# Prompt queries and probabilities turned by plain transposes that write their PSUM tile from the last column to the first

## The chip, the cores and the metric

The kernel runs on one NeuronCore of one Trainium2 chip. The metric is the device time of one execution in microseconds (us), lower is better; the number that stands for a kernel is the median of several runs.

## What is computed

One inference step of a hybrid decoder layer, on 256 prompt tokens and 64 sample tokens (8 sequences of 8), with a model width of 2048, all in float32. Cut to what matters here:

```python
z = einsum("bsd,dc->bsc", rms_norm(x, g_mix), w_in)      # one wide projection
q, k = rms_norm(z_q, g_qb), rms_norm(z_k, g_kb)          # 16 heads of 64
# attention of the prompt, patterns (window, dilation) = (128,1), (512,4), (2048,16)
sc = einsum("brnqhe,brnkhe->brnhqk", q, k) * scale + bias[t5_bucket(distance)]
p  = exp(sc - max(sc)); o = einsum("...qk,...ke->...qe", p / sum(p), v)
# sample tokens: the same against a cache of 2048 past keys and values
# further: gMLP spatial gate, cross-attention into 256 memory tokens
h  = x + concat(ya, yb, ym) @ w_out
y  = h + hier_moe(rms_norm(h, g_ffn))                    # top-1 of 4 groups, top-2 of 8 experts
```

The bias of the window attention depends only on the distance between query and key.

## The kernel before, in words

The program is written engine by engine; each engine runs its instructions in the written order and waits on semaphores. There are three stages. First the memory projection. Then a loop over `UNITS_X` = 108 units `s` of the input projection (nine chunks of 512 columns, four quarters of the weights each, three row groups), with all attention work hung between the units at fixed places. Last the output projection and the mixture of experts, whose weights are streamed through a ring.

The projections use a seven-product scheme per 2x2 block: TensorE runs `plain_products` and `mixed_products` (L620) for the prompt rows and `small_unit` (L612) for the sample rows; VectorE mixes the weights (L1408 to L1424) and adds the products (L1435 to L1446). Weight blocks come over the SP queue (L402), cached keys and values too (L467, L472).

Attention needs operands turned (transposed). `turn(n)` is called 24 times: `kind = n // 4` says what is turned (0 memory keys, 1 and 3 prompt and sample queries, 2 and 4 keys, 5 memory queries), `w` which 128 columns. For kinds 1 and 3 the two tiles of prompt queries (`t < 2`) must come out with the queries in reverse order, because the window bias is read from memory by a DMA whose rows step forwards by one element while the distance has to fall; so the scores have their query rows reversed, and the probabilities are reversed back when `pair_turn` turns them. Scalar engine copies each turned tile out of PSUM (L1225 for `turn`, L1239 for `pair_turn`).

In the kernel before, a reversing turn is an ordinary matmul with the data as left operand and the constant `flip`, the identity with its rows in reverse order, as right operand. A turn without reversal is `nc.tensor.transpose` with the identity (here `tr`). A group of heads is handled in pairs: `pair_scores(p)` at `s = PAIR_AT[p]`, `pair_turn(p)` two units later, `pair_values(p)` three units later; the sample sequences are handled by `qk` (L780, L786), `turn_s` (L796) and `pv` (L813). The places are given by two tables:

```python
PAIR_AT = (37, 41, 45, 49, 71, 75, 79, 83)
TURN_AT = [10, 11, 12, 13, 19, 20, 21, 22, 30, 31, 32, 33, 61, 61, 62, 62, 66, 66, 67, 67, 91, 91, 92, 92]
```

Of the kernel before, what the change touches and what calls it, by code (L numbers as in the profile page):

```python
# [29 lines left out]
P = 128  # L30
# [40 lines left out]
def sample_step(s):  # L71

    for n, at in enumerate(START):
        if at <= s < at + 7:
            return n, s - at
    return None, None
# [17 lines left out]

CST = {}
_at = 0
for _n, _w in (("ident", 128), ("gx", 16), ("flip", 128), ("ones", 128), ("ltri", 128), ("iota", 64),
               ("gmix", 16), ("gmem", 16), ("bs", 4), ("bss", 4), ("gff", 16), ("wr", KT * 36), ("wst", 4 * 128), ("wsbd", 4 * 64),
               ("wmask", 256), ("wsel", 32), ("mmask", 512), ("msel", 32)):
    CST[_n] = (_at, _w)  # L100
    _at += _w
# [19 lines left out]
def hybrid_step(nc, x_rows, mem_rows, x_t, mem_t, w_proj, w_o, kc, vc, mkc, mvc, cst_d, gv_d,  # L121
                relb_d, onehot_d, w_gu, w_dn, mst_d, o_y, o_k, o_v, o_va, o_mk, o_mv,
                bias_d, bias_q_d):
    with ExitStack() as ctx:
        def sb(name, shape, dt=F32):
            return ctx.enter_context(nc.sbuf_tensor(name, shape, dt))
# [5 lines left out]
        cst = sb("cst", [P, NCST])  # L132
# [5 lines left out]
        ps = ctx.enter_context(nc.psum_tensor("ps", [P, 8, 512], F32))  # L138

        def c(name, rows=P):  # L140
            a, w = CST[name]
            return cst[0:rows, a:a + w]

        def area(at, *dims):
            n = int(np.prod(dims))
            ap = arena[:, at:at + n]
            if len(dims) == 1:
                return ap
            names = "abcdef"[:len(dims)]
            return ap.rearrange(f"p ({' '.join(names)}) -> p {' '.join(names)}",  # L150
                                **{k: v for k, v in zip(names, dims)})

        ident = c("ident")
# [54 lines left out]
        sc_p = [area(A_SP + 512 * b, 512) for b in range(3)]  # L208
# [42 lines left out]
        def field(t, at, *dims):  # L251
            n = int(np.prod(dims))
            names = "abcdef"[:len(dims)]
            return t[:, at:at + n].rearrange(f"p ({' '.join(names)}) -> p {' '.join(names)}", **{k: v for k, v in zip(names, dims)})
# [4 lines left out]
        pw = field(cst, done + 6 * P + 1024, 3, P)  # L259
        pwT = field(cst, done + 6 * P + 1024, NT)  # L260
        assert done + 9 * P + 1024 <= NCST
        pm = field(cst, CST["flip"][0], 3, P)
        actT = field(stat, 184, 2, SLOTS)

        mst = gv[:, 0:NMST]
# [328 lines left out]
        def _(pe):  # L594
            mm, tr = nc.tensor.matmul, nc.tensor.transpose
# [58 lines left out]
            for k in range(K4):  # L654
                pe.wait_ge(w_first[k], 16)
                pe.wait_ge(mem_scaled, k + 1)
                for t in range(2):
                    last = mm(ps[:, t, :], memT[:, k, t * P:(t + 1) * P], wring[:, 0, k, :], start=k == 0, stop=False)
                    if k == K4 - 1:
                        last.then_inc(unit_done, 1)  # L660
            for i in range(1, 2 * QTR):
# [9 lines left out]
                if i == QTR - 1:  # L671
                    pe.wait_ge(s_relb, 32)
                    for n in range(4):
                        last = mm(ps[32 * n:32 * n + H, 6, :], relb[:, :], onehot[:, n * 512:(n + 1) * 512], start=True, stop=True)
# [3 lines left out]
            pe.wait_ge(s_cst, 32)  # L678
            pe.wait_ge(tab_cp, TABLE // 512)

            def turn(n):
                kind, w = n // 4, n % 4
                pe.wait_ge(normed, (1, 2, 3, 4, 5, 6)[kind])
                if n == 0:
                    pe.wait_ge(z_ready, 4)
                if n == 12:
                    pe.wait_ge(y_used, 4)
                if n == 20:
                    pe.wait_ge(y_used, 8)
                if n >= 2:  # L690
                    pe.wait_ge(tr_used, n - 1)
                for t in range(2 if kind == 0 else 3):
                    if kind == 0:
                        src = mk[:, t, w * P:(w + 1) * P]
                    else:
                        src = z[:, (Z_QK, Z_KQ, Z_QK, Z_KQ, Z_QM)[kind - 1], t, w * P:(w + 1) * P]
                    if kind in (1, 3) and t < 2:
                        last = mm(ps[:, 3 + n % 2, t * P:(t + 1) * P], src, c("flip"), start=True, stop=True)
                    else:
                        last = tr(ps[:, 3 + n % 2, t * P:(t + 1) * P], src, ident)  # L700
                last.then_inc(tr_done, 1)

            def pair_scores(p):
# [11 lines left out]
            def pair_turn(p):  # L715

                pe.wait_ge(sc_read, 2 * p + 2)
                for k in range(2):
                    pe.wait_ge(p_ready, 2 * p + k + 1)
                    for a in range(0, 384, 128):  # L720
                        last = mm(ps[:, 3 + k, a:a + 128], sc_p[k][:, a:a + 128], c("flip"), start=True, stop=True)
                    last.then_inc(pt_mm, 1)

            def pair_values(p):
# [155 lines left out]
            for s in range(UNITS_X):  # L880
                ch, q, t = s // 12, s // 3 % QTR, s % 3
# [10 lines left out]
                n, i = sample_step(s)  # L892
# [41 lines left out]
                for p, at in enumerate(PAIR_AT):  # L934
                    if s == at + 2:
                        pair_turn(p)
                for k, at in enumerate(TURN_AT):
                    if s == at:
                        turn(k)
# [57 lines left out]
            for t in range(3):  # L997
                last = tr(ps[:, 7, t * 36:(t + 1) * 36], lgT[:, t * P:(t + 1) * P], ident[0:36, 0:36])
# [376 lines left out]
        def _(dve):  # L1375
# [113 lines left out]
            def squares_of(k):  # L1489
                src, groups, e, _, scratch, need = norms[k]  # L1490
                if k == 1:
                    dve.wait_ge(po, 2)
                if k == 5:
                    dve.wait_ge(st_v[0], 32)
                    dve.wait_ge(spv_mm, 12)
                    dve.wait_ge(pv_mm, 4)
                dve.wait_ge(z_ready, need)
                V.tensor_tensor(scratch, src, src, ALU.mult).then_inc(squared, 1)

            def sums_of(k):  # L1500
                _, groups, e, _, scratch, _ = norms[k]
                dve.wait_ge(squared, k + 1)
                link(V.tensor_reduce(st_n[:, 0:groups], scratch.rearrange("p n (h e) -> p (n h) e", e=e), X, ALU.add))
                V.tensor_scalar(st_n[:, 0:groups], st_n[:, 0:groups], 1.0 / e, EPS, ALU.mult, ALU.add).then_inc(ms_ready, 1)  # L1504
                state["n"] += 1

            def scale_by_root(k):
                src, groups, e, _, _, _ = norms[k]
                dve.wait_ge(rs_ready, state["n"])
                hh = COLS // e  # L1510
                for t in range(src.shape[1]):
                    v = src[:, t].rearrange("p (h e) -> p h e", e=e)
                    last = V.tensor_tensor(v, v, st_nr[:, t * hh:(t + 1) * hh].unsqueeze(2).to_broadcast([P, hh, e]), ALU.mult)
                last.then_inc(rooted, 1)
# [499 lines left out]
def distance_bucket(dist):  # L2014

    d = np.maximum(dist, 0)
    exact = 16
    df = np.maximum(d, 1).astype(np.float32)
    large = exact + (np.log(df / np.float32(exact)) / np.float32(math.log(2048 / exact)) * np.float32(16)).astype(np.int32)
    return np.where(d < exact, d, np.minimum(large, 31))  # L2020


def constants():

    dist = DIST0 - np.arange(TABLE)
    count = sum(((dist >= 0) & (dist <= w) & (dist % dl == 0)).astype(int) for w, dl in ((128, 1), (512, 4), (2048, 16)))
    onehot = np.zeros((33, TABLE), np.float32)
    onehot[distance_bucket(dist), np.arange(TABLE)] = 1
    onehot[32] = np.where(count > 0, np.log(np.maximum(count, 1)), NEG)
    c = {n: np.zeros((P, w), np.float32) for n, (_, w) in CST.items()}  # L2030
    c["ident"][:] = np.eye(P)
    c["flip"][:] = np.eye(P)[::-1]
    c["ones"][:] = 1
    c["ltri"][:] = np.triu(np.ones((P, P)), 1)
    c["iota"][:] = np.arange(64)
    h, q = np.divmod(np.arange(P), NQ)
    c["wmask"][:] = (h % 4)[:, None] == np.arange(256) // DH
    c["wsel"][:] = h[:, None] // 4 * NQ + q[:, None] == np.arange(32)
    b, h = h // G, h % G
    c["mmask"][:] = h[:, None] == np.arange(512) // DG  # L2040
    c["msel"][:] = b[:, None] * NQ + q[:, None] == np.arange(32)
    m = np.zeros((P, NMST), np.float32)
    m[:, 0:128] = np.arange(1, 129)
    m[:, 128:160] = (np.arange(P) % 32)[:, None] == np.arange(32)
    m[:, 160:160 + NTHR] = SLOTS * np.arange(1, NTHR + 1)
    return onehot, c, m
# [86 lines left out]
```

## Time and profile before

| | |
|---|---|
| median of 3 runs | 1121.97 us (1121.44 to 1122.15) |
| the profiled execution: its time | 1128.33 us |
| the profiled execution: its span | 1126.4 us |
| TensorE matmul busy | 1039.1 us, 92% of the span |
| VectorE busy | 546.9 us, 49% |
| ScalarE busy | 202.6 us, 18% |
| mean granted TensorE clock | 0.986 of full speed |
| DMA | 384.54 MB, mean 341 GB/s |

The span is the time from the first to the last instruction of the profiled execution. Shares of busy time are averages over stages with different limits, so they have to be read with the stage in mind: the input projection with the attention lies from about 100 to 500 us, the output projection from about 500 to 665 us, the experts after that.

### The profile page before, as it was taken

Reading aid. Unit: us, or ns where it says so; the run is one execution under the profiler, and the core shown is the slowest. Engines: PE = TensorE matmul, PEld = TensorE weight load, DVE = VectorE, ACT = ScalarE, POOL = GpSimd, SP = SyncE. Lnnn points to the kernel's source line nnn. Section 1 sums busy time; section 2 is a strip of 40 time slices with the busy share of each in tenths; the row PEclk is TensorE's granted clock in tenths of the full one; section 3 lists DMA queues with packets and bytes.
Section 4 is the critical chain, followed back from the end, with each engine's and each line's share of the span. In section 5 each row is a group of like instructions: output and inputs, shape, how many; then the busy total and the mean of one; then the engine's idle time right before and its main releaser. Section 6 shows DMA issues by size and latency. Waiting matters only on the chain.

```text
span 1126.4 us, 17412 instructions
## 1 busy us (share of the span) xinstructions
PE 1039.1 (92%) x7225; PEld 589.5 (52%) x7225; DVE 546.9 (49%) x1076; ACT 202.6 (18%) x463; POOL 43.1 (4%) x40
## 2 busy tenths in 40 slices
PE   8998999999999999999999998998996879787887
PEld 3686876666666666677777543333332323232232
DVE  3765555555544566475534135544443434343432
ACT  1022103131212331311101112121211111111112
POOL 0030110001100000000000000000000000000000
PEclk9998999999999999999999999999999999998999
DMA  9899648989999999733957459999999999999995
GB/s 323 341 280 262 246 152 350 358 338 348 352 415 410 380 358 367 306 143 119 336 216 279 169 221 388 429 415 428 427 428 427 427 429 428 429 428 427 427 426 223
DMA packets 38981, 384.54 MB, mean 341 GB/s; under 512 B 4911, under 2 KB 7599, under 8 KB 10895
## 3 DMA queue, kind: packets, MB, share of 16 engines
q1 hardware_dynamic: 36336, 375.83, 83.4%
q0 software_dynamic: 1568, 5.62, 2.0%
q10 hardware_dynamic: 1008, 2.10, 0.5%
q8 instruction: 52, 0.85, 0.3%
q14 instruction: 17, 0.14, 0.0%
HBM read 375.63 MB, written 7.90 MB: 340 GB/s over the span
## 4 chain that ended last, share of the span: by engine, by line
PE 68%; DMA 20%; DVE 7%; ACT 2%; issue 2%; POOL 0%; SPq 0%; ACTq 0%; DVEq 0%; POOLq 0%
PE ps L620 24%; DMA arena<-w_gu 15%; PE ps L612 7%; PE ps L1092 6%; PE ps L1019 5%; PE ps L1130 4%; PE ps L813 4%; PE ps L1111 3%; PE ps L602 3%; PE ps L780 3%; DMA arena<-x_rows 3%; DMA arena<-w_proj 2%; DVE cst L1900 1%; PE ps L1135 1%; PE ps L796 1%
## 5 line engine op out<-in xcount | busy, mean ns | idle before, releaser
L620 PE MATMUL ps<-arena 128*128 128x256 f32 x1456 | 333.7, 384 | 4.4 <-DVE arena L1435 4.4
L620 PEld LDWEIGHTS ps<-arena 128*128 128x128 f32 x1456 | 272.3, 191 | 53.4 <-issue 17.3
L1092 PE MATMUL ps<-arena,cst 128*32 128x512 f32 x1024 | 127.0, 631 | 30.7 <-DMA arena<-w_gu 29.1
L1900 DVE STREAM_TRANSPOSE cst<-ps 128x512 f32<-128x512 f32 x31 | 22.2, 717 | 177.0 <-PE ps L1019 177.0
L612 PE MATMUL ps<-arena 128*64 128x256 f32 x832 | 101.3, 385 | 0.0
L1092 PEld LDWEIGHTS ps<-arena,cst 128*32 128x32 f32 x1024 | 32.3, 113 | 115.8 <-issue 77.9
L1019 PE MATMUL ps<-arena,cst 128*32 128x512 f32 x768 | 90.6, 605 | 0.5 <-DVE cst L1829 0.5
L1111 PE MATMUL ps<-arena,stat 128*32 128x512 f32 x512 | 61.6, 598 | 23.3 <-DVE stat L1904 23.2
L612 PEld LDWEIGHTS ps<-arena 128*64 128x64 f32 x832 | 55.1, 136 | 38.5 <-issue 15.4
L1408 DVE TENSOR_TENSOR arena<-arena 128x512 f32<-128x512 f32 x52 | 35.7, 687 | 54.7 <-PE ps L620 39.5
L1930 DVE COPY arena<-ps 32x512 f32<-32x512 f32 x62 | 42.9, 691 | 38.7 <-PE ps L1111 37.4
L1019 PEld LDWEIGHTS ps<-arena,cst 128*32 128x32 f32 x768 | 26.0, 115 | 63.9 <-issue 62.6
L1130 PE MATMUL ps<-arena,cst 128*128 128x512 f32 x112 | 49.9, 598 | 9.2 <-ACT cst L1365 9.2
L1892 DVE TENSOR_TENSOR arena<-ps,arena 128x512 f32<-128x512 f32 x64 | 44.0, 691 | 20.9 <-PE ps L1130 18.4
L1340 ACT COPY gv<-ps 128x512 f32<-128x512 f32 x32 | 18.7, 585 | 188.2 <-PE ps L1092 188.2
L602 PE MATMUL ps<-arena 128*128 128x512 f32 x112 | 49.7, 596 | 1.2 <-DMA arena<-w_proj 0.8
L1362 ACT COPY arena<-ps 32x512 f32<-32x512 f32 x62 | 35.6, 575 | 76.9 <-PE ps L1111 76.1
L1101 PEld LDWEIGHTS ps<-gv 128*128 128x128 f32 x256 | 31.1, 191 | 26.5 <-issue 26.0
L1963 POOL TENSOR_TENSOR stat<-stat,nhalf 128x24 f32<-128x24 f32 (+4 forms) x10 | 26.6, 2655 | 477.4 <-DVE stat L1504 324.0
L813 PE MATMUL ps<-arena 128*32 128x256 f32 (+1 forms) x704 | 44.0, 383 | 0.1
L780 PE MATMUL ps<-arena 128*32 128x512 f32 (+1 forms) x384 | 39.3, 527 | 0.9 <-issue 0.6
L1424 DVE TENSOR_TENSOR arena<-arena 128x512 f32<-128x512 f32 x52 | 36.0, 692 | 6.4 <-PE ps L620 2.3
(286 smaller groups left out, 973.0 us busy)
## 6 DMA issues: line engine op xcount, KB each, us to landing
arena<-w_gu SPq DMA_DIRECT2D x64, 2048.0 KB, 29.6
arena<-w_dn SPq DMA_DIRECT2D x32, 2048.0 KB, 28.5
arena<-w_proj SPq DMA_DIRECT2D x43, 1024.0 KB, 7.8
arena<-kc SPq DMA_DIRECT2D x16, 2048.0 KB, 10.3
arena<-vc SPq DMA_DIRECT2D x16, 2048.0 KB, 9.6
arena<-w_o SPq DMA_DIRECT2D x16, 1024.0 KB, 4.9
arena<-kc SPq DMA_DIRECT2D x8, 1024.0 KB, 9.1
arena<-vc SPq DMA_DIRECT2D x8, 1024.0 KB, 10.0
```

The lines of the kernel that those rows point to most:

```text
L602: last = mm(ps[:, bank + t, :], src[:, kt, r0:r0 + m], wring[:, i % SLOTS_W, k, :], start=first and k == 0, stop=final and k == K4 - 1)
L612: last = mm(ps[64 * j:64 * j + 64, bank, col:col + HALF], src[:, kt, NPROMPT:NT], wring[:, i % SLOTS_W, k, HALF * j:HALF * j + HALF], star ...
L620: last = mm(psum[:, regions(v)[j - 1]], left[a], right[:, a], start=first and opens and a == 0, stop=final and a == 1, skip_group_check=True)
L780: last = mm(ps[32 * g:32 * g + 32, 6, 0:w], qpad[:, e * 128 + 32 * g:e * 128 + 32 * g + 32], kp[j][:, e, :], start=half == 0, stop=half == 1)
L813: last = mm(ps[32 * g:32 * g + 32, 5, 0:256], pt_s[0:w, t, 32 * g:32 * g + 32], v, start=t == 0, stop=t == VT)
L1019: last = mm(ps[32 * j:32 * j + 32, 1, :], pm[:, t, 32 * s:32 * s + 32], hres[:, t, 512 * j:512 * j + 512], start=t == 0, stop=t == 2)
L1092: last = mm(ps[g:g + 32, 0, :], xgT[:, s % 2, kt, :], w[:, k, :], start=kt < 4, stop=kt >= KT - 4)
L1111: last = mm(ps[32 * g:32 * g + 32, 3, :], actT[:, j, :], w[:, j, 512 * g:512 * g + 512], start=j == 0, stop=j == 1)
L1130: mm(ps[:, 4 + n, :], pwT[:, t * P:(t + 1) * P], y4[:, 512 * n:512 * n + 512], start=True, stop=True).then_inc(comb_mm, 1)
L1424: V.tensor_tensor(wmix[:, 3], b21, wmix[:, 1], ALU.subtract).then_inc(w_mixed, 1)
L1892: V.tensor_tensor(yres[:, t, cols], ps[:, bank + n, :], before[:, t, cols], ALU.add).then_inc(added[t], 1)
L1930: V.tensor_copy(y4[32 * b:32 * b + 32, 512 * g:512 * g + 512], ps[32 * g:32 * g + 32, 3, :]).then_inc(ye_copied, 1)
```

## The change

The reversing matmuls are replaced by transposes with the identity, and the reversal moves to where the result is written: `backward(bank, a)` builds an access pattern for the same 128 columns of PSUM that starts at the last column and has a step of -1. The constant `flip` is no longer made; its place among the constants stays (now `slots`, zeros), since a later tensor (`pm`) lies there. No instruction is added, dropped or moved on any engine, and no wait changes: the engines issue the same calls in the same order, and only the form of 64 calls on TensorE is another.

```diff
-for _n, _w in (("ident", 128), ("gx", 16), ("flip", 128), ("ones", 128), ("ltri", 128), ("iota", 64),
+for _n, _w in (("ident", 128), ("gx", 16), ("slots", 128), ("ones", 128), ("ltri", 128), ("iota", 64),
...
-        pm = field(cst, CST["flip"][0], 3, P)
+        pm = field(cst, CST["slots"][0], 3, P)
...
+            def backward(bank, a):
+
+                (step, rows), (one, _) = ps[:, bank].ap
+                return bass.AP(tensor=ps[:, bank].tensor, offset=ps[:, bank].offset + a + P - 1, ap=[[step, rows], [-one, P]])
...
-                    if kind in (1, 3) and t < 2:
-                        last = mm(ps[:, 3 + n % 2, t * P:(t + 1) * P], src, c("flip"), start=True, stop=True)
-                    else:
-                        last = tr(ps[:, 3 + n % 2, t * P:(t + 1) * P], src, ident)
+                    out = backward(3 + n % 2, t * P) if kind in (1, 3) and t < 2 else ps[:, 3 + n % 2, t * P:(t + 1) * P]
+                    last = tr(out, src, ident)
...
-                        last = mm(ps[:, 3 + k, a:a + 128], sc_p[k][:, a:a + 128], c("flip"), start=True, stop=True)
+                        last = tr(backward(3 + k, a), sc_p[k][:, a:a + 128], ident)
...
-    c["flip"][:] = np.eye(P)[::-1]
```

## Rows read from the trace of the kernel before

**Rows 1.** The page: busy time by engine, and the span in 40 slices

```profile
PE 1039.1 (92%) x7225; PEld 589.5 (52%) x7225; DVE 546.9 (49%) x1076; ACT 202.6 (18%) x463; POOL 43.1 (4%) x40
...
PE   8998999999999999999999998998996879787887
...
DMA  9899648989999999733957459999999999999995
```

**Rows 2.** Stretches: us, busy by engine, granted clock, DMA share, GB/s

```profile
98.00:105.00 7.00, 4.89 (x12) 3.94 (x13) 5.06 (x9) 4.16 (x9) 0.88 (x1) 0.51 1.00 290
105.00:645.00 540.00, 534.49 (x3896) 377.17 (x3895) 285.47 (x597) 108.23 (x283) 29.36 (x17) 1.00 0.78 300
645.00:690.00 45.00, 39.99 (x247) 18.35 (x249) 20.07 (x84) 8.28 (x18) 0.88 (x1) 1.00 0.62 247
690.00:1120.00 430.00, 369.14 (x2715) 130.10 (x2708) 178.50 (x290) 68.46 (x140) 0.00 (x0) 0.97 0.98 416
```

**Rows 3.** The chain that ended last, in order: start, us, what (around reversing turns)

```profile
125.49 0.45 PE ps L698 x4
125.94 0.11 PE ps L700
126.05 1.88 PE ps L612 x16
...
194.41 1.34 PE ps L721 x12
195.75 3.46 PE ps L620 x16
...
490.44 0.11 PE ps L754
```

**Rows 4.** All matmuls of three lines: duration min/median/max in ns, first and last start

```profile
L698 PE MATMUL ps<-cst,arena x32: 272/275/377, 125.3 to 306.3; 128*128 128x128 f32 x32
L721 PE MATMUL ps<-cst,arena x96: 275/275/377, 194.2 to 422.6; 128*128 128x128 f32 x96
L700 PE MATMUL ps<-cst,arena x52: 272/273/330, 93.1 to 456.2; 128*128 128x128 f32 x52
```

**Rows 5.** TensorE in order of time: start, length of the group, count

```profile
166.51 0.49 PE L700 MATMUL ps<-cst,arena 128*128 128x128 f32 x3
166.84 0.60 PE L620 MATMUL ps<-arena 128*128 128x256 f32 x2
324.20 0.88 PE L700 MATMUL ps<-cst,arena 128*128 128x128 f32 x6 [0.55 <-DVE arena L1529]
324.92 0.60 PE L620 MATMUL ps<-arena 128*128 128x256 f32 x2
```

**Rows 6.** The chain where it leaves TensorE, from 142 and from 245 us

```profile
135.72 0.11 PE ps L700
...
140.93 1.31 PE ps L620 x6
...
148.04 4.17 POOL stat L1963
...
155.53 1.82 DVE arena L1529 x3
...
157.39 0.55 PE ps L700 x3
...
245.34 0.06 PE ps L713
...
252.63 0.61 DVE arena L1585
...
253.38 1.92 PE ps L780 x16
255.30 1.53 PE ps L721 x12
256.84 3.46 PE ps L620 x16
```

**Rows 7.** VectorE mixing weights beside the turn at 255 us

```profile
254.66 0.69 DVE L1424 TENSOR_TENSOR arena<-arena 128x512 f32<-128x512 f32 x1
```

**Rows 8.** Keys loaded at 305 us, their landing, and their first matmuls

```profile
305.09 11.98 SPq L467 DMA_DIRECT2D arena<-kc  x3
...
DMA to landing us min/median/max: 10.7/13.7/14.0
...
L780 PE MATMUL ps<-arena x48: 379/592/617, 321.7 to 333.7; 128*32 128x512 f32 x32, 128*32 128x256 f32 x16
```

**Rows 9.** The experts: first loads on the SP queue, and the chain's longest pieces

```profile
664.65 0.80 SPq L531 DMA_DIRECT2D arena<-w_dn  x2
668.36 0.33 SPq L529 DMA_DIRECT2D arena<-w_gu  x1
...
1077.45 28.00 DMA arena<-w_gu
```

## The prediction

> **What bounds the kernel now.** I read the page first: TensorE is busy 92% of the span, and its slices stand at 9 in nearly all of the first two thirds, while the DMA slices reach a steady 9 only in the last third [rows 1]. So the limit changes on the way, and the next view is the table of stretches. From 105 to 645 us TensorE is busy 534.49 of 540 us at full clock, with DMA at 0.78: that stretch is bound by TensorE. From 690 to 1120 us DMA is at 0.98 and TensorE at 369 of 430 us: that one is bound by the expert weights [rows 2]. All reversing turns lie from 125 to 423 us [rows 4], so in the first kind of stretch. The chain that ended last confirms it: it goes through the very matmuls that the change edits, both in `turn` (L698) and in `pair_turn` (L721) [rows 3]. What they get shorter by is on the path there.
>
> **What the change does, step by step.** The edited calls are 64: in `turn`, kinds 1 and 3 are eight turns with two reversed tiles each, 16 tiles; `pair_turn` is called eight times with six tiles each, 48 tiles. The trace shows 32 matmuls for the 16 calls of L698 and 96 for the 48 calls of L721, so an ordinary float32 product of a tile runs as two passes. L700, a transpose, shows 52 matmuls for its 8 + 8 + 36 calls: one pass each [rows 4].
>
> Price of a pass. The duration of one is 272 to 275 ns in both forms [rows 4], but passes overlap, so what counts is the distance from one to the next. Reversing: 12 passes of L721 take 1.34 us of the chain, 4 passes of L698 take 0.45 us: 112 ns each, 224 ns a tile [rows 3]. Transposing: from the first of three L700 to the matmul behind them 166.84 - 166.51 = 0.33 us, 110 ns a tile, and a single L700 or L754 stands with 0.11 us in the chain [rows 3, 5]. The six at 324.20 us take 0.72 us to the next matmul, 0.12 us each, the first of them straight behind a wait [rows 5]. I take 109 to 110 ns a tile.
>
> The sum: a pair turn goes from 1.34 to 6 x 0.109 = 0.65 us, 0.69 us less, times 8 is 5.5 us. A query turn goes from 0.45 + 0.11 to 3 x 0.109 us, 0.23 us less, times 8 is 1.85 us. Together 7.3 us, or 64 x 115 ns. Nothing else has a cost: no instruction and no wait is added, the constants have the same size, and the copies L1225 and L1239 read the same columns.
>
> The unknown term is the write from the last column to the first; no row of the trace has one. Bounds: below, 109 ns a tile, as the forward transposes; a gain beyond that is excluded, since the same columns are streamed. Above I take twice that, 218 ns, each written column costing two steps instead of one; 64 x (224 - 218) leaves 0.4 us of gain. All rows of passes have about 0.85 ns a column, in either form and with the plain product delivering sums instead of moved data, so the pace follows what is streamed in, and the order in which addresses are counted out looks like a matter of one number in the pattern. I take the lower bound.
>
> The Trainium skill (TensorE: Matmul & The Clock Gate, Part 4, PE-mode transpose) gives about 275 ns for a transpose inside a kernel. The trace agrees as far as the duration of a single one goes, 273 ns. Were that the cost in the stream, the sum would be 64 x (224 - 275), 3.3 us slower; the distance of 110 ns between neighbours says that it is not.
>
> **Does it arrive at the end?** Where the chain leaves TensorE, I looked at what started the detour and whether a reversing turn lies in its shadow. From 142 to 157.4 us it runs over VectorE and GpSimd (square sums, the power on GpSimd at 148.04, the scaling L1529) and begins behind a matmul of L620 that ends at 142.24 us; the query turns before it are done by 135.8 us, so it only begins earlier. From 245.3 to 253.4 us it runs over VectorE, from the scores L713 to the keys' product L780; the turn at 255.30 us comes behind it [rows 6]. Next late could be the mixing of weights on VectorE: the pair turn at 255 us is followed by products that want the blocks of L1424, whose last ends at 255.35 us, while the turn would end at 256.84 - 0.69 = 256.15 us: 0.8 us are left [rows 6, 7]. That one is the closest I found; I allow 0.1 us for such small waits. The keys of 305 us are the tightest load: the first lands about 14 us after 305.09, at 319.1 us at the latest, and is used at 321.7 us [rows 8]. Between issue and use lie at most two query turns (the last at 306.3 us [rows 4]) that shrink by 0.46 us together, against 2.6 us of slack. The issue itself waits for TensorE and moves with it.
>
> The expert stage does not get shorter, it starts earlier. Its stream of loads starts with the issues at 664.65 and 668.36 us, which wait for TensorE's use of the ring and for the router's work, and before them DMA is not full (0.62 from 645 to 690 us) [rows 2, 9]. So it begins some 7 us sooner and ends as much sooner.
>
> The profiled execution took 1128.33 us with a span of 1126.4; less 7.3 it would be 1121.0. The median of the runs is 6.36 us below it, which no row divides; I carry the saving over whole: 1121.97 - 7.3 = 1114.7 us, 0.65% faster. A measurement of this kernel tells about 0.2% (2.2 us) from no change.
>
> **Rivals.** (1) Part of the gain is hidden: a VectorE chain or a load takes over after some of the turns. For it speaks that VectorE's mixing ends only 0.8 us ahead at 255 us, and DMA is at 0.78 on average [rows 2, 7]; against it that I found slack at each place. If a third to a half of the pair turns' 5.5 us goes to new waits, 1116.5 to 1117.5 us; at the worst 1119.5. Chance 0.09.
>
> (2) The backward write costs a second step a column: 218 ns a tile, 1121.6 us, no change. Nothing in the profile shows it or excludes it. Chance 0.08.
>
> (3) The other side: the backward write breaks the stream, each tile ends before the next begins. Then a tile costs its whole duration, 273 ns [rows 4], and 64 x (273 - 224) = 3.1 us is lost: 1125.1 us; it decides from 224 ns a tile on, and with a write that restarts at every column (four steps, 436 ns) it would be 13.6 us, 1135.6 us. Against it: forward transposes overlap fully. Chance 0.06.
>
> (4) The clock falls. At 98 to 105 us, after TensorE had waited, its clock was 0.51, that is 1.2 instead of 2.4 GHz [rows 2]; such a stretch loses some 3.4 us. Were each pair turn followed by one, the kernel would be 8 x 3.4 - 7.3 = 20 us slower, 1142 us; two of them take back 6.8 of the 7.3 us. Against it: six transposes in a row at 324 us, and those of L754, lie in stretches at full clock, between dense products [rows 2, 3, 5]. Chance 0.02. The Trainium skill (same page and part) says that transposes do not count as activity for the clock; by that rule 0.65 us of transposes would be a gap of that length, and the trace has one of that length, at 324 us, without a fall.
>
> **How the numbers follow.** The forecast, all of the gain within 0.8 us: 0.75, range 1114.2 to 1115.5. With (1) the faster cases have 0.84 and reach to 1119.5. Case (2) is the same: 0.08. Cases (3) and (4) are slower: 0.08. The range 1113.8 to 1119.5 holds 0.84 and leaves out (2) to (4); its lower end allows the copies and waits 0.9 us of gain more than I can name.
>
> **What would show it.** Right: L721's line shows 48 matmuls instead of 96 and the line of `turn` 68 for all its tiles; a pair turn stands with 0.65 us in the chain; the distance between neighbours is 110 ns; TensorE's busy time in the stretch falls by some 7 us; the experts' first loads are issued 7 us earlier, and their stage is as long as before. Wrong: distances of 218 ns or more (rivals 2, 3); a clock below 1 near the turns (4); new idle time of TensorE before L620 behind L1424, or before L780 and L813 behind loads (1).

## The result and the profile after

The changed kernel has a median of 1115.34 us (20 runs, 1113.03 to 1124.86) against 1122.24 us of the kernel before (20 runs, 1120.71 to 1127.06). The ratio is 0.9944 with a 95% interval of 0.9932 to 0.9956, that is 6.3 us less, 4.9 to 7.6. A ratio is not the quotient of the two medians, which would be 0.9938 here, 6.9 us less. The ratios leave out one run, of the kernel with only the query turns changed, which took 1140.11 us at a granted clock of 0.946. Measured a second time, beside the last experiments, it gave 0.9941 (0.9928 to 0.9954). The 1114.7 us predicted lie inside both, and so does the full gain of 7.3 us (0.9935).

The page after answers to [rows 1]. Its columns are the same: busy us (share) and instructions, then the slices.

```profile
PE 1028.2 (93%) x7161; PEld 579.9 (52%) x7161; DVE 546.5 (49%) x1076; ACT 201.3 (18%) x463; POOL 43.6 (4%) x40
...
PEclk9999999999999999999999999999998999999999
```

TensorE has 7161 instead of 7225 matmuls: 64 passes are gone, one for each reversed tile, and as many weight loads. All matmuls of the two lines (L703 is `turn` now, L724 `pair_turn`), duration min/median/max, answer to [rows 4]:

```profile
L703 PE MATMUL ps<-cst,arena x68: 272/273/329, 93.2 to 441.7; 128*128 128x128 f32 x68
L724 PE MATMUL ps<-cst,arena x48: 272/273/329, 186.3 to 408.1; 128*128 128x128 f32 x48
```

48 and 68 passes for 48 and 68 tiles. The chain after, in order of time (start, us, what), at the places of [rows 3] and [rows 6]:

```profile
118.53 0.33 PE ps L703 x3
118.86 1.88 PE ps L612 x16
120.73 0.48 PE ps L703 x3
...
186.49 0.66 PE ps L724 x6
187.14 3.46 PE ps L620 x16
...
243.35 1.92 PE ps L783 x16
245.27 0.81 PE ps L724 x6
246.08 3.46 PE ps L620 x16
```

A query turn went from 0.56 to 0.33 us, the first pair turn from 1.34 to 0.66 and the one behind the keys' product from 1.53 to 0.81 us. The neighbours are unchanged, 1.88 us for the 16 matmuls of L612 and 3.46 for those of L620. The stretches, to set beside [rows 2]:

```profile
98.00:105.00 7.00, 7.00 (x42) 5.38 (x41) 4.83 (x7) 2.57 (x6) 0.00 (x0) 1.00 1.04 437
105.00:637.00 532.00, 526.50 (x3809) 367.07 (x3808) 281.87 (x594) 107.07 (x283) 29.76 (x17) 1.00 0.77 300
...
690.00:1120.00 430.00, 355.25 (x2588) 125.33 (x2580) 173.88 (x281) 64.88 (x133) 0.00 (x0) 0.97 0.96 405
```

The clock is 1.00 all through the stretch with the turns. The first row shows something that has nothing to do with the change: in the profile before TensorE stood still for 4.4 us, until 100.1 us, and ran at half clock afterwards; in this one it did not. The first reversing turn starts at 125 us in the profile before, so no edited call lies ahead of the stop. The two spans, 1126.4 and 1111.2 us, therefore differ by 15.2 us, much more than the medians. In the chain before, the standstill goes back to the third tile of `x_rows`:

```profile
82.31 14.44 DMA arena<-x_rows
...
98.77 0.48 ACT arena L1182
...
99.27 0.70 DVE arena L1435
...
100.11 5.26 PE ps L620 x12
```

The Scalar engine squares this tile before it copies the first chunk's products out of PSUM, and TensorE waits for that PSUM. So the spans can't be compared as they are. Two marks leave out the start and the expert stage: the first product of the cached keys, and the experts' first gather. In the order of time, first the kernel before:

```profile
170.39 1.92 PE L780 MATMUL ps<-arena 128*32 128x512 f32 x16
...
675.82 2.78 PE L1019 MATMUL ps<-arena,cst 128*32 128x512 f32 x24 [0.48 <-DVE cst L1829]
```

and the changed kernel:

```profile
162.46 1.92 PE L783 MATMUL ps<-arena 128*32 128x512 f32 x16
...
661.30 2.78 PE L1022 MATMUL ps<-arena,cst 128*32 128x512 f32 x24 [0.48 <-DVE cst L1832]
```

505.43 us before, 498.84 after: 6.59 us less. Between the marks lie the 48 tiles of the pair turns and the last 8 of the query turns; 56 x (224 - 109) ns is 6.44 us. Added up as they stand in the chain, the eight pair turns take 11.38 us before and 5.75 us after, 5.63 less instead of 5.5, which with the 0.92 us of four query turns comes to 6.55. The other 8 tiles, 0.92 us by the price, lie ahead of the first mark. From the start of the first reversing turn to this mark it is 44.90 us in the chain before (125.49 to 170.39) and 43.93 in the chain after (118.53 to 162.46), 0.97 us less, so they arrive too. The loads of the expert stage are issued earlier by what TensorE is earlier (compare [rows 9]: 664.65 and 668.36 us), 14.5 us in this pair of profiles:

```profile
650.14 0.80 SPq L531 DMA_DIRECT2D arena<-w_dn  x2
653.85 0.33 SPq L529 DMA_DIRECT2D arena<-w_gu  x1
```

### The profile page after: what moved, and what is told of

Same layout as the page of the kernel before. It is cut to its first block, busy times and chain, and to the rows that moved or that the text cites. A ratio compares the mean times of both kernels' runs of the same rounds, so it can differ in the third digit from the quotient of the medians.

```text
span 1111.2 us, 17284 instructions
## 1 busy us (share of the span) xinstructions
PE 1028.2 (93%) x7161; PEld 579.9 (52%) x7161; DVE 546.5 (49%) x1076; ACT 201.3 (18%) x463; POOL 43.6 (4%) x40
## 4 chain that ended last, share of the span: by engine, by line
PE 74%; DMA 15%; DVE 7%; ACT 2%; issue 1%; POOL 0%; SPq 0%; ACTq 0%; DVEq 0%; POOLq 0%
PE ps L620 27%; DMA arena<-w_gu 13%; PE ps L612 7%; PE ps L1095 7%; PE ps L1022 5%; PE ps L1133 4%; PE ps L1114 4%; PE ps L816 4%; PE ps L602 3%; PE ps L783 3%; DMA arena<-w_proj 2%; DVE cst L1903 1%; DVE cst L1836 1%; PE ps L1138 1%; PE ps L799 1%
## 5 line engine op out<-in xcount | busy, mean ns | idle before, releaser
L620 PE MATMUL ps<-arena 128*128 128x256 f32 x1456 | 331.2, 382 | 0.0
L620 PEld LDWEIGHTS ps<-arena 128*128 128x128 f32 x1456 | 270.6, 190 | 48.1 <-issue 12.7
L612 PE MATMUL ps<-arena 128*64 128x256 f32 x832 | 101.3, 385 | 0.0
L612 PEld LDWEIGHTS ps<-arena 128*64 128x64 f32 x832 | 55.1, 136 | 38.6 <-issue 15.9
L1895 DVE TENSOR_TENSOR arena<-ps,arena 128x512 f32<-128x512 f32 x64 | 44.0, 691 | 20.9 <-PE ps L1133 18.5
L1427 DVE TENSOR_TENSOR arena<-arena 128x512 f32<-128x512 f32 x52 | 36.0, 692 | 6.4 <-PE ps L620 2.2
```

What stands on the lines that cost most here:

```text
L612: last = mm(ps[64 * j:64 * j + 64, bank, col:col + HALF], src[:, kt, NPROMPT:NT], wring[:, i % SLOTS_W, k, HALF * j:HALF * j + HALF], star ...
L620: last = mm(psum[:, regions(v)[j - 1]], left[a], right[:, a], start=first and opens and a == 0, stop=final and a == 1, skip_group_check=True)
L1427: V.tensor_tensor(wmix[:, 3], b21, wmix[:, 1], ALU.subtract).then_inc(w_mixed, 1)
L1895: V.tensor_tensor(yres[:, t, cols], ps[:, bank + n, :], before[:, t, cols], ALU.add).then_inc(added[t], 1)
```

## The experiments

The theory: a transpose is one pass of 109 ns and the ordinary product two of 112; the backward write is free; all of it is on TensorE's path. The main rivals: the backward write has a price, the gain comes from something other than the form, and part of it is hidden.

**Forward writes.** All 64 calls stay transposes, but write forwards.

```diff
-                    out = backward(3 + n % 2, t * P) if kind in (1, 3) and t < 2 else ps[:, 3 + n % 2, t * P:(t + 1) * P]
+                    out = ps[:, 3 + n % 2, t * P:(t + 1) * P]
...
-                        last = tr(backward(3 + k, a), sc_p[k][:, a:a + 128], ident)
+                        last = tr(ps[:, 3 + k, a:a + 128], sc_p[k][:, a:a + 128], ident)
```

> The changed kernel with its 64 transposes writing from the first column to the last, so queries and probabilities aren't reversed (the window attention of the prompt is computed with wrong pairs). My theory, the write in reverse costs nothing: the same time as the changed kernel, 0.9935 of before, and 109 ns between neighbours. Rival, each column written backwards costs something: this kernel is faster than the changed one, at 5 ns a tile by 0.3 us, at 100 ns by 6.4 us.

Measured: 1115.26 us, ratio 0.9949 (0.993 to 0.9967). Between the two marks 498.84 us, to the hundredth what the backward writes need in the first profile of the changed kernel. The direction costs nothing that these two profiles can tell, and at 1 ns a tile it would be 0.06 us.

**Only the pair turns, only the query turns.** In the first, the line of `turn` stays as before and `pair_turn` is changed; in the second the other way round.

```diff
-                        last = mm(ps[:, 3 + k, a:a + 128], sc_p[k][:, a:a + 128], c("flip"), start=True, stop=True)
+                        last = tr(backward(3 + k, a), sc_p[k][:, a:a + 128], ident)
```

> Only the 48 tiles of the pair turns are changed. Theory, the gain adds up tile by tile: 48 x 115 ns = 5.5 us less, 0.995 of before. Rival, part of it is hidden behind VectorE or a load: less than 4.5 us, with new idle time of TensorE in the profile.

Measured: 1118.27 us, ratio 0.9958 (0.9942 to 0.9973), 4.7 us less (3.0 to 6.5).

> Only the 16 tiles of the query turns are changed. Theory: 16 x 115 ns = 1.85 us less, 0.9984 of before. Rival, the query turns are hidden behind the wait near 95 us or the VectorE chain from 142 us: no change, and the starts of later products in the trace don't move by 1.85 us.

Measured: 1121.35 us, ratio 0.999 (0.998 to 0.9999), 1.1 us less (0.1 to 2.2). The gains add up to 5.8 us by the ratios (4.8 us by the medians); the intervals reach 1.1 to 1.8 us to either side. The marks are sharper: 504.51 us with the query turns alone, 0.92 us less for the 8 tiles between them, as computed. For the 8 tiles ahead of the first mark the rival was that the wait near 95 us or the VectorE chain from 142 us hides them. It is out: from the first matmul of the first query turn to the first mark it is 44.2 us here and 44.1 to 44.2 in the other profiles with shorter query turns, against 45.1 to 45.2 in those with the query turns as before. With the pair turns alone 501.58 us, 3.85 us less, where 48 tiles should give 5.5. This profile has something new: TensorE waited 1.8 us for keys until 315 us, and 0.5 us at another place.

**The reversing matrix in a transpose.** The constant `flip` stays the right operand and the write goes forwards, but the call is a transpose.

```diff
-                        last = mm(ps[:, 3 + k, a:a + 128], sc_p[k][:, a:a + 128], c("flip"), start=True, stop=True)
+                        last = tr(ps[:, 3 + k, a:a + 128], sc_p[k][:, a:a + 128], c("flip"))
```

> The reversing matrix stays the right operand and the write goes forward, but the call is a transpose. Theory, the gain comes from the one pass of the transpose form and from nothing in the write: the same as the changed kernel, 0.9935 of before, 109 ns between neighbours. Rival, the gain needs the plain identity (or the reversed write): two passes or a slower pace.

Measured: 1117.8 us, ratio 0.9952 (0.9936 to 0.9969). All matmuls of its `pair_turn`, then the waits of TensorE between 296 and 322 us (who waited for what: us, times, longest), and the chain there:

```profile
L721 PE MATMUL ps<-cst,arena x48: 272/273/329, 187.7 to 412.3; 128*128 128x128 f32 x48
...
PE ps L780 <- DMA arena<-kc: 2.7, 1, 2.7
...
295.29 18.92 DMA arena<-kc
...
314.25 1.92 PE ps L780 x16
```

48 passes of the same length, and a pair turn stands with 0.66 to 0.81 us in its chain, as in the changed kernel: the one pass comes with the transpose form, and a matrix that reverses does as well in it as the identity. The backward write is one of two ways to have the reversal, not the source of the gain. In this profile, too, TensorE waited for the keys: they were issued at 295.29 us and took 18.9 us. That wait, 3.3 us in all, makes up the 3.2 us that the marks lie further apart than in the changed kernel (502.02 against 498.84 us).

**Four forms, five times each.** Each tile of a pair turn is turned five times in the same place; the form depends on the pair.

```diff
-                        last = mm(ps[:, 3 + k, a:a + 128], sc_p[k][:, a:a + 128], c("flip"), start=True, stop=True)
+                        for _ in range(5):
+                            if p < 2:
+                                last = tr(backward(3 + k, a), sc_p[k][:, a:a + 128], ident)
+                            elif p < 4:
+                                last = tr(ps[:, 3 + k, a:a + 128], sc_p[k][:, a:a + 128], ident)
+                            elif p < 6:
+                                last = mm(ps[:, 3 + k, a:a + 128], sc_p[k][:, a:a + 128], c("flip"), start=True, stop=True)
+                            else:
+                                last = mm(backward(3 + k, a), sc_p[k][:, a:a + 128], ident, start=True, stop=True)
```

> Each tile of a pair turn is turned five times in the same place, in four forms: pairs 0 and 1 transposed with the write in reverse, 2 and 3 transposed forwards (these come out unreversed, so their attention is wrong), 4 and 5 as before by the reversing matrix, 6 and 7 by an ordinary product with the identity that writes in reverse. Theory: 109 ns a tile for both transposes, 224 ns for both ordinary products, so the direction of the write is free in either form. Rival: the reverse forms are slower than the forward ones, seen in the distance between neighbours.

One run, 1151.83 us. Its chain, with one pair turn of each form (L728 transpose backwards, L730 transpose forwards, L732 product forwards, L734 product backwards):

```profile
190.15 3.27 PE ps L728 x30
...
234.10 3.28 PE ps L730 x30
...
362.11 6.78 PE ps L732 x60
...
440.98 6.70 PE ps L734 x60
```

30 transposes take 3.27 us backwards and 3.28 forwards, 109 ns each; the other pair turn of either kind stands with 3.42 us. 60 passes of the product take 6.70 and 6.78 us forwards, 6.70 and 6.90 backwards, 112 to 115 ns each, 223 to 230 a tile. It is the disputed price measured by itself, 30 times in a row: for the transposes it is the same in both directions, and for the products the two pair turns of one direction differ by more than the directions do. Between the marks it is 534.50 us, 29.07 more than before; 24 x (5 x 109 - 224) + 24 x 4 x 224 ns would be 29.2.

**Each reversing product twice.** The kernel before, with every one of the 64 products done two times.

```diff
-                        last = mm(ps[:, 3 + k, a:a + 128], sc_p[k][:, a:a + 128], c("flip"), start=True, stop=True)
+                        for _ in range(2):
+                            last = mm(ps[:, 3 + k, a:a + 128], sc_p[k][:, a:a + 128], c("flip"), start=True, stop=True)
```

> The kernel before with each reversing product done twice. Theory, all of this time is on the path: 64 x 224 ns = 14.3 us more, 1.0128 of before. Rival, waits elsewhere absorb part: clearly less than 14.3 us.

Measured: 1136.15 us, ratio 1.0122 (1.01 to 1.0145), 13.7 us more (11.2 to 16.3). Between the marks 517.92 us, 12.49 more, for 56 x 224 ns = 12.54. In this direction all of it is on the path and none is absorbed.

**The squares of the third tile later.** This one follows the standstill at 95 us, in the changed kernel and in the one before: the Scalar engine squares the third tile after it has copied the first chunk's products, and VectorE takes the sums at unit 11 instead of 9.

```diff
-            for t in range(3):
+            for t in range(2):
                 tile_sums(2 + t, NORM_X + t)
...
                 if s == 11:
+                    tile_sums(4, NORM_X + 2)
                     act.wait_ge(rs_ready, 3)
...
-                if s == 9:
+                if s == 11:
                     x_sums = stat[:, NORM_X:NORM_X + 3]
```

> The changed kernel, but the Scalar engine squares the third tile of x_rows after the first chunk's products are copied out of PSUM, and VectorE takes the sums two units later. Theory: the stop of TensorE at 95 us, which the profile before has and the one after hasn't, comes from the landing of this tile and is behind most of the spread of runs; this kernel never has it: 3 to 8 us faster than the slow ones among the changed kernel's runs, median about 1113, 0.992 of before, and a smaller spread. Rival, the spread comes from the expert stage: the same median and spread as the changed kernel.

Measured: 1117.49 us (1113.07 to 1121.65), ratio 0.9941 (0.9919 to 0.9964). Neither the median of 1113 us nor the smaller spread came.

> The same shift of the squares in the kernel before, with its reversing products. Theory: with the stop at 95 us gone in both, the distance between this one and the changed kernel with late squares is the change alone, 7.3 us. Rival, the change also alters the start: another distance.

Measured: 1121.75 us, ratio 0.9986 (0.9974 to 0.9998). The distance between the two kernels with late squares is 4.3 us by the medians and about 5 us by the ratios, not 7.3, though the intervals are too wide to rule 7.3 out. The theory that the stop is behind the spread fell. The change of order is worth 1.6 us (0.2 to 2.9) in the kernel before and nothing that can be told in the changed one, where the runs spread as widely as without it. (In the kernel before they lie within 3.7 us, 12 runs, against 7.0 us, 17 runs, without it.) The standstill is real, but of the profiles without this move only the one of before shows it at 4.4 us; in the others TensorE waited at most 1.1 us there. The profile of the changed kernel with late squares has the wait for keys again, 2.9 us, and behind it a clock of 0.91 from 300 to 320 us.

**The keys ahead of a weight block.** Three of the profiles with shorter pair turns had TensorE's matmuls wait 1.8 to 2.9 us for the keys of sequence 4; of those with the pair turns as before or longer one had 0.4 us, the others none. At unit 62 the SP queue issues a weight block of 1 MB and then these keys, 2 MB; here the order is exchanged.

```diff
                 if s % 3 == 2:
                     sp.wait_ge(unit_done, UNITS_M + s + 1)
-                    weights(11 + s // 3)
+                    if s != START[3] + 4:
+                        weights(11 + s // 3)
...
                     keys(n + 1, i - 4)
+                    if s == START[3] + 4:
+                        weights(11 + s // 3)
```

> The changed kernel with one transfer moved: at unit 62 the keys of sequence 4 (2 MB) are issued ahead of the weight block (1 MB) that stood before them. Theory, with the turns shorter these keys land late in part of the executions (TensorE waited 2.7 us for them in two profiles with all turns shorter, 1.8 us in the one with only the pair turns changed, not in the ones with the pair turns as before), which costs about 1 us of the 7.3 on average: they land some 2.4 us sooner, the profile has no wait for them, and the median is 0.5 to 1.5 us below the changed kernel's. Rival, the wait is only exchanged for one on the weight block: the same median.

Measured: 1115.6 us, ratio 0.9947 (0.9932 to 0.9961). The profile has no wait for keys; its issues at that place and the time of the keys to landing:

```profile
294.37 0.33 SPq L467 DMA_DIRECT2D arena<-kc  x1
294.75 0.43 SPq L402 DMA_DIRECT2D arena<-w_proj  x1
```

The keys landed 13.5 us after their issue, against 16.0 us in the changed kernel's first profile and 16.5 in its second. They are issued no earlier, 131.5 us after the first mark against 131.4; it is the weight block that now starts behind them, 2.3 us later by the same measure.

> The same exchange in the kernel before. Theory: there the keys land in time anyway, so no change (within 0.5 us of before). Rival, the kernel before also waits for them at times: up to 1 us faster.

Measured: 1122.57 us, ratio 1.0 (0.999 to 1.0011), between the marks 505.40 us: nothing, as expected, though the keys landed after 11.0 us.

> The changed kernel with the keys ahead of the weight block and the late squares of the third tile. Theory: both small waits gone, the best version so far, about 1113.5 us, 0.992 of before. Rival: the late squares bring nothing, the same as with the keys alone.

Measured: 1116.92 us, ratio 0.9947 (0.9932 to 0.9962), between the marks 498.84 us.

> The changed kernel itself, beside the others on the same chip, so that the small differences are read against it: 0.9944 of before as in its first measurement. If the two moves are worth anything, it is slower than both by 0.5 us or more, and its profile shows at unit 66 either a small wait for keys or one of 2 to 3 us.

Measured: 1116.48 us, ratio 0.9941 (0.9928 to 0.9954), between the marks 499.28 us with a wait of 0.3 us for keys (and 0.7 us at the weight load there, that is, where the left operand is loaded into TensorE). So neither move can be told in the medians of one sitting: 1115.6 with the keys first, 1116.92 with both moves and 1116.48 us without lie closer together than their intervals are wide. The keys first have the median 0.9 us lower, as the theory had it, but the ratio not (0.9947 against 0.9941), and with both moves it is higher; the 1113.5 us expected of both were missed by 3.4. That the exchange lands the keys sooner is seen (13.5 and 13.4 us in its two profiles of the changed kernel); that it brings time is not shown, and the version to keep is the changed kernel as it is.

The distances between the two marks in all profiles, with the wait of TensorE's matmuls for keys in between:

| kernel | marks, us | less than before | wait for keys |
|---|---|---|---|
| before | 505.43 | | none |
| changed | 498.84 | 6.59 | none (0.3 at the weight load) |
| changed, again | 499.28 | 6.15 | 0.3 (1.0 at the weight load) |
| forward writes | 498.84 | 6.59 | none (0.3 at the weight load) |
| reversing matrix in a transpose | 502.02 | 3.41 | 3.3, of which 2.7 at 314 us |
| pair turns alone | 501.58 | 3.85 | 2.3, of which 1.8 at 315 us |
| query turns alone | 504.51 | 0.92 | 0.4 |
| four forms, five times each | 534.50 | -29.07 | none |
| products twice | 517.92 | -12.49 | none |
| changed, late squares | 502.80 | 2.63 | 2.9 |
| before, late squares | 505.42 | 0.01 | none |
| changed, keys first | 498.82 | 6.61 | none |
| before, keys first | 505.40 | 0.03 | none |
| changed, both moves | 498.84 | 6.59 | none |

## Why the prediction was right

**The terms of the sum.** 224 ns for a reversing product, 109 for a transpose, 64 tiles: every one of them was measured close to what was computed, 0.66 and 0.33 us for the two kinds of turn in the chain, and 3.27 us for 30 transposes in a row. The sum was a little small: the prediction took the pair turn of 1.34 us for all eight, while four of them stand with 1.42 to 1.54 us and save 0.72 to 0.74. With 5.63 us for the pair turns and 1.9 for the query turns (0.92 and 0.97 us) the gain on the path is 7.5 us, not 7.3. The pace had to be read from the distance between neighbours, not from the 272 to 275 ns that either form lasts; by the durations alone one pass saved would have looked like 273 ns.

**The unknown term.** The backward write was priced at nothing, with 218 ns as the upper bound. Forward writes (498.84 us between the marks, the same) and the four forms (3.27 against 3.28 us) show that it is free. Rivals (2) and (3) of the prediction are out by the same rows. One supporting sentence of the prediction was misread: not all rows of passes have about 0.85 ns a column. L620 has (3.46 us for 16 passes of 256 columns), but the 16 passes of 256 columns of L612 take 1.88 us, 0.46 ns a column [rows 3]. The price did not rest on it.

**The clock.** Rival (4) is out: the clock is 1.00 from 105 to 637 us in the changed kernel, with all its reversing turns in that stretch. In the kernel with five turns per tile it is 1.00 from 180 to 450 us too:

```profile
180.00:450.00 270.00, 267.42 (x2313) 188.89 (x2309) 131.24 (x316) 60.95 (x172) 10.94 (x6) 1.00 0.86 336
```

There four groups of 30 transposes last 3.3 to 3.4 us each. The Trainium skill (TensorE: Matmul & The Clock Gate, Part 4, PE-mode transpose) says that transposes do not count as activity; the trace shows no fall after any of these groups (1.00 from 180 to 450 us), but dense products stand on both sides of each, so the rule itself is neither confirmed nor refuted.

**Whether it arrives at the end.** The detours over VectorE stayed what they were. At 245 us VectorE's mixing (L1427) ended at 245.32 us and the pair turn at 246.08 us: 0.8 us were left, as worked out. The expert stage starts earlier and lasts 443.8 to 446.7 us from its first gather to the end of the last matmul in all profiles, changed or not.

**The part that was mis-sized** is the sentence on the keys of 305 us, "against 2.6 us of slack". The distance from issue to use came out as worked out: 16.6 us before and 16.2 with shorter query turns, waits taken off. The time to land was the error; it was taken, 14.0 us, from one execution. The same load took 13.5, 14.6, 16.1 and 16.6 us in the other profiles with the pair turns as before or longer, and 15.8, 16.0, 16.5, 18.5, 18.9 and 19.1 us in those with the pair turns shorter. So the slack was never 2.6 us to be relied on. In these profiles the load took longer with the pair turns shorter, but the two groups overlap (15.8 to 16.6 us). A reason would be that the transfers asked for in this stretch are pressed together where DMA has no room; that is argued, not shown, for the DMA share from 295 to 310 us is 1.01 to 1.03 in eight profiles with either kind of turn. In three of six profiles the slack was overdrawn by 1.8 to 2.9 us. This is rival (1), a load that takes over, in some executions. The waits of the six profiles for keys, at all places, are 0, 0, 0.3, 2.3, 2.9 and 3.3 us, 1.5 us on average, which would explain why the ratios give 6.3 and 6.6 us and not 7.3 to 7.5; but the intervals reach to 7.6 us and more, and the exchange of the keys, which removed the wait from the profile, brought nothing that can be told. That it takes these 1.5 us of the median is argued, not shown. Why the landing differs by 3 us between executions of one kind stays open. That 1115.34 us lies even in the narrow range of the forecast, 1114.2 to 1115.5, is luck in part: a sum that was 0.2 us small and a wait that was not foreseen offset each other, and the second measurement, 1116.48 us, lies outside of it.

**The spread of runs**, 1113 to 1125 us, was not foreseen. Three places vary from one profile to the next: the start (the first mark lies at 162.5 to 170.4 us), the wait for keys, and the expert stage (3 us). The late squares were an attempt on the first of them, and failed to narrow it.

## What to carry to other kernels

In float32, an ordinary product with a permutation matrix cost two passes of TensorE here (224 ns a 128x128 tile) and the transpose form one (109 ns), so every product that only moves data is worth a look; a reversal can go into either the matrix or the access pattern of the output. Price a pass by the distance to its neighbour in a dense stretch, not by its duration. And take the slack of a load from several executions: one profile showed 2.6 us where five others had a wait.

## What the runs showed of the hardware

- A step of -1 in TensorE's output pattern cost nothing, for a transpose (109 ns a 128x128 float32 tile either way) as, within 0.2 us in 60 passes, for an ordinary product (6.70 and 6.90 us backwards, 6.70 and 6.78 forwards).
- A float32 transpose with a reversing permutation in place of the identity ran at the pace of the plain one (48 passes of 273 ns, 0.66 us for six) and delivered the reversed tile.
- The same 2 MB load at the same place of the program took 13.5 to 16.6 us to land in five profiles with the old or longer pair turns, and 15.8 to 19.1 us in six with shorter ones.
- 30 float32 transposes in a row (3.3 us) between dense products left the granted clock at 1.00.
